# A hybrid diffusion block on one core: SyncE issues the modulation-piece transfers, TensorE sums their rows one tile later, and the last full down blocks are finished in pairs

## The reference

```python
ml = (silu(c) @ w_ada + b_ada).reshape(B, 9, D)          # nine modulation vectors, latent
mc = (silu(c_ctx)[None] @ w_ada + b_ada).reshape(1, 9, D) # the same for the context
h  = h  + 0.5*ml[:,2] * swiglu(modulate(rmsnorm(h,  g0), ml[:,0], ml[:,1]), ffn_w_in0, ffn_w_out0)
hc = hc + 0.5*mc[:,2] * swiglu(modulate(rmsnorm(hc, g0), mc[:,0], mc[:,1]), ffn_w_in0, ffn_w_out0)
# then: token mixing (pooling group and gated DeltaNet group), output projection,
# a second SwiGLU FFN on h alone, final RMSNorm
```

## Time and profile before

| What | Value |
|---|---|
| Median of three runs | 2981.55 us (2976.54 to 2985.0) |
| Profiled execution, its own time | 2979.76 us |
| Span of its trace | 2978.0 us |
| TensorE matmul busy | 2858.0 us, 96% of the span |
| VectorE busy | 1633.4 us, 55% |
| ScalarE busy | 968.1 us, 33% |
| GpSimd busy | 237.9 us, 8% |
| Mean granted TensorE clock | 0.977 |

### The profile page before, as it was taken

The page is one execution under the profiler, slowest core; times in us unless marked ns, Lnnn a source line. Parts: engine busy times, 40 slices in busy tenths (PEclk is TensorE's granted clock), DMA queues, the critical chain, the costliest instruction groups (busy, mean ns, idle before and its releaser), DMA issues. The chain is left out here.

```text
span 2978.0 us, 47625 instructions
## 1 busy us (share of the span) xinstructions
PE 2858.0 (96%) x17840; PEld 2496.2 (84%) x17840; DVE 1633.4 (55%) x2197; ACT 968.1 (33%) x1443; POOL 237.9 (8%) x388
## 2 busy tenths in 40 slices
PE   6999999999998999999999999998999999999998
PEld 3687777777877787888888888888999999999998
DVE  2556666666666663223222766665666555555555
ACT  2222221222212122111212555554444434443344
POOL 3000000000000000000101011546220000000001
PEclk8999999999999999999999999999999999999999
DMA  9765666667787874554554376686646555555554
GB/s 363 269 207 180 206 194 194 192 192 219 268 276 273 292 271 167 195 193 162 195 193 148 91 206 190 185 239 204 188 151 190 183 188 185 185 181 183 187 187 148
DMA packets 410321, 604.42 MB, mean 203 GB/s; under 512 B 52960, under 2 KB 303840, under 8 KB 401520
## 3 DMA queue, kind: packets, MB, share of 16 engines
q1 hardware_dynamic: 361536, 417.42, 44.4%
q10 hardware_dynamic: 48688, 185.73, 18.4%
HBM read 560.02 MB, written 43.02 MB: 203 GB/s over the span
## 5 line engine op out<-in xcount | busy, mean ns | idle before, releaser
L1929 DVE TENSOR_TENSOR wl<-raw,wh 128x1024 fp32r<-128x1024 f32 x638 | 781.4, 1231 | 997.6 <-ACT wh L1455 995.6
L1455 ACT CAST wh<-raw 128x1024 fp32r<-128x1024 f32 x638 | 664.7, 1047 | 1564.1 <-PE ps L760 1121.5
L759 PE MATMUL ps<-xl,wh 128*128 128x512 f32 (+1 forms) x2560 | 973.8, 380 | 0.0
L758 PE MATMUL ps<-xh,wh 128*128 128x512 f32 (+1 forms) x1904 | 728.1, 382 | 3.2 <-DVE xl L1980 2.5
L760 PE MATMUL ps<-xh,wl 128*128 128x512 f32 (+1 forms) x1904 | 720.8, 379 | 0.0
L759 PEld LDWEIGHTS ps<-xl,wh 128*128 128x128 f32 x2560 | 485.9, 190 | 90.8
L758 PEld LDWEIGHTS ps<-xh,wh 128*128 128x128 f32 x1904 | 362.2, 190 | 86.5 <-issue 15.8
L760 PEld LDWEIGHTS ps<-xh,wl 128*128 128x128 f32 x1904 | 361.2, 190 | 67.4
L758 PE MATMUL ps<-x2h,wh 128*128 128x256 f32 x1408 | 395.4, 281 | 1.7 <-DVE x2l L1980 1.7
L759 PE MATMUL ps<-x2l,wh 128*128 128x256 f32 x1408 | 393.8, 280 | 0.0
L760 PE MATMUL ps<-x2h,wl 128*128 128x256 f32 x1408 | 393.8, 280 | 0.0
(11 more groups left out here) (274 smaller groups left out, 2675.9 us busy)
## 6 DMA issues: line engine op xcount, KB each, us to landing
raw<-in_ffn_w_in SPq DMA_DIRECT2D x704, 256.0 KB, 3.3
raw<-in_ffn_w_out SPq DMA_DIRECT2D x176, 512.0 KB, 3.7
abuf<-in_w_ada ACTq DMA_DIRECT2D x64, 1024.0 KB, 7.1
abuf<-in_w_ada ACTq DMA_DIRECT2D x96, 512.0 KB, 4.2
xl<-d_h ACTq DMA_DIRECT2D x80, 512.0 KB, 3.3
ada_t<-in_ada SPq DMA_DIRECT2D x64, 512.0 KB, 9.1
raw<-in_w_in SPq DMA_DIRECT2D x128, 256.0 KB, 3.4
raw<-in_w_out SPq DMA_DIRECT2D x32, 512.0 KB, 4.5
```

Of the source, the lines that this page charges most:

```text
L758: mm(out, ah, bh, start=first, stop=False, skip_group_check=reopened)
L759: mm(out, ah, bl, start=False, stop=False, skip_group_check=reopened)
L1455: nc.scalar.copy(wh[:, t % HL, :], raw[:, t % RAW, :]).then_inc(hi_done, 1)
L1929: tt(tl, raw[:, t % RAW, :], th.bitcast(F32), ALU.subtract).then_inc(lo_done, 1)
```

## The change

Three things. (1) `load_piece` goes from ScalarE's stream to SyncE's: step x-1 of the running piece is issued behind weight tile x, and step 15 behind tile 0 of the next group (for the last piece, behind the first down tile). ScalarE's wait for the transfer of the hidden pair two back, in front of `hidden`, is replaced by a wait for the pair one back, in front of the next pair's transfer; only the last pair keeps one in front of `hidden`. (2) TensorE calls `reduce_rows` after tile 12 instead of 11, and `reduce_columns` after tile 14 instead of 13; VectorE's program is unchanged. (3) In the second half of the down projection blocks 0 and 1, then 2 and 3, are finished in pairs (`ff_both`): for each closing tile both blocks, and in the first pair the wait for a tile stands in front of that tile rather than in front of all.

```diff
--- before.py
+++ after.py
@@ -71,7 +71,6 @@
 PIECE_ONE = (N_MOD - 5) * D // (2 * HALF)
 PIECES = PIECE_BOTH + PIECE_ONE
 PIECE_AT = 12
-LOAD_AT = PIECE_AT - 2
 assert PIECES == GROUPS - 1
 
 
@@ -554,6 +553,25 @@
             def up_load(r, m, x):
                 load(r, UP_TILES, m * UP_TILES + x, up_source(0, r, m, *divmod(x, K_TILES)))
 
+            def load_piece(r, n, i):
+
+                sp.wait_ge(acc_done, steps(r, n, i - 1))
+                if n < PIECE_BOTH:
+                    src = w_ada_v[:, i, ds(r * HALF + (2 * D + n * HALF), HALF)]
+                    sp.dma_start(abuf[:, i % 2, 0, :], src).then_inc(abuf_in[i % 2], 16)
+                else:
+                    src = w_ada_v[:, i, ds(r * (2 * HALF) + (5 * D + (n - PIECE_BOTH) * 2 * HALF), 2 * HALF)]
+                    sp.dma_start(abuf[:, i % 2].rearrange("p s n -> p (s n)"), src).then_inc(abuf_in[i % 2], 16)
+
+            def up_loads(r, m):
+
+                for x in range(UP_TILES):
+                    up_load(r, m, x)
+                    if x:
+                        load_piece(r, m - 1, x - 1)
+                    elif m > 1:
+                        load_piece(r, m - 2, KT - 1)
+
             def ff_load(r, t, block, a):
 
                 sp.wait_ge(lo_done, tiles(r, HR, t))
@@ -575,13 +593,18 @@
                     up_load(0, 0, i - 3)
             for x in range(ADA_SS - 3, UP_TILES):
                 up_load(0, 0, x)
-            with sp.Fori(0, GROUPS - 1) as r:
-                for x in range(UP_TILES):
-                    up_load(r, 1, x)
+            up_loads(0, 1)
+            with sp.Fori(0, PIECE_BOTH - 1) as r:
+                up_loads(r, 2)
+            up_loads(0, PIECE_BOTH + 1)
+            with sp.Fori(0, PIECE_ONE - 1) as r:
+                up_loads(r, PIECE_BOTH + 2)
             for a in range(2):
                 t = T_DOWN + a * HALF_TILES
                 for i in range(HELD):
                     ff_load(0, t + i, SPILLED * 2 + i, a)
+                    if a == 0 and i == 0:
+                        load_piece(0, PIECES - 1, KT - 1)
                 with sp.Fori(0, (HALF_TILES - HELD) // HR) as r:
                     for b in range(HR):
                         ff_load(r, t + HELD + b, b, a)
@@ -910,13 +933,22 @@
                     n = ff_part(a, i, c, slice(0, NTOK))
                 n.then_inc(tile_used, 1)
 
-            def ff_whole(a, c, tiles_):
+            def ff_whole(c, tiles_):
                 for i in tiles_:
-                    n = ff_part(a, i, c, slice(0, NTOK), i == tiles_[-1])
-                    if a == 0 and c == 7:
+                    n = ff_part(0, i, c, slice(0, NTOK), i == tiles_[-1])
+                    if c == 7:
                         n.then_inc(tile_used, 1)
-                if a or c < 7:
+                if c < 7:
                     n.then_inc(down_done[0], 1)
+
+            def ff_both(c, tiles_):
+                for i in tiles_:
+                    if c == 0:
+                        ff_arrived(0, 1, i)
+                    for b in range(2):
+                        n = ff_part(1, i, c + b, slice(0, NTOK), i == tiles_[-1])
+                        if i == tiles_[-1]:
+                            n.then_inc(down_done[0], 1)
 
             def down():
                 pe.wait_ge(F[0]["hf_done"], 2 * GROUPS * PAIRS - 2)
@@ -930,10 +962,13 @@
                     for i in range(HALF_TILES - HR, HALF_TILES - close):
                         ff_tile(0, a, i)
                     closing_tiles = range(HALF_TILES - close, HALF_TILES)
-                    for i in closing_tiles:
-                        ff_arrived(0, a, i)
-                    for c in range(8 if a == 0 else 4):
-                        ff_whole(a, c, closing_tiles)
+                    if a == 0:
+                        for i in closing_tiles:
+                            ff_arrived(0, a, i)
+                        for c in range(8):
+                            ff_whole(c, closing_tiles)
+                for c in range(0, 4, 2):
+                    ff_both(c, closing_tiles)
                 for c in range(4, 8):
                     for i in closing_tiles:
                         n = ff_part(1, i, c, slice(0, SEQ), i == closing_tiles[-1])
@@ -992,9 +1027,9 @@
                         if p == 0 and m >= 2:
                             pe.wait_ge(red_out, r * 2 + 2 * (m - 1))
                     up_tile(0, r, m * UP_TILES + x, p, k)
-                    if x == PIECE_AT - 1:
+                    if x == PIECE_AT:
                         reduce_rows(r, m - 1)
-                    elif x == PIECE_AT + 1:
+                    elif x == PIECE_AT + 2:
                         reduce_columns(r, m - 1)
 
             def group(f, r, s, base, x_base):
@@ -1495,39 +1530,27 @@
                     i = fn(XH[n // 2][:, k, c_], ub[:, k % 2, c_], ACT.Identity, bias=SHIFT[n][s][:, k:k + 1])
                 i.then_inc(xh_done, 1)
 
-            def load_piece(r, n, i):
-
-                act.wait_ge(acc_done, steps(r, n, i - 1))
-                if n < PIECE_BOTH:
-                    src = w_ada_v[:, i, ds(r * HALF + (2 * D + n * HALF), HALF)]
-                    act.dma_start(abuf[:, i % 2, 0, :], src).then_inc(abuf_in[i % 2], 16)
-                else:
-                    src = w_ada_v[:, i, ds(r * (2 * HALF) + (5 * D + (n - PIECE_BOTH) * 2 * HALF), 2 * HALF)]
-                    act.dma_start(abuf[:, i % 2].rearrange("p s n -> p (s n)"), src).then_inc(abuf_in[i % 2], 16)
-
             def up_pairs(r, m, before=None):
 
                 for x in range(UP_TILES):
                     if before is not None:
                         before(x)
                     split(r, UP_TILES, m * UP_TILES + x + AHEAD)
-                    if x < LOAD_AT and m:
-                        load_piece(r, m - 1, x + KT - LOAD_AT)
-                    elif x >= LOAD_AT and m < GROUPS - 1:
-                        load_piece(r, m, x - LOAD_AT)
                     if x == 2 and m:
                         hidden_out(r, m, -1)
                     elif x == K_TILES + 2 and m < GROUPS - 1:
                         hidden_out(r, m, 0)
                     if x % K_TILES == K_TILES - 1:
                         p = x // K_TILES
-                        if m:
-                            act.wait_ge(hid_out, r * (64 * PAIRS // 2) + 32 * (2 * m + p - 1))
+                        if m == GROUPS - 1 and p:
+                            act.wait_ge(hid_out, 32 * SPILLED)
                         hidden(0, r, m, tiles(r, UP_TILES, m * UP_TILES + x), p, hth)
 
             def hidden_out(r, m, p):
 
                 n, b = 2 * m + p, 2 * (p % 2)
+                if n:
+                    act.wait_ge(hid_out, r * 64 + 32 * n)
                 act.wait_ge(F[0]["h_ready"], r * GROUP_FF + 2 * (n + 1))
                 rows = slice(2 * n, 2 * n + 2) if isinstance(r, int) else ds(r * GROUP_FF + 2 * n, 2)
                 for part, src in enumerate((hth, htl)):
```

## The result

| What | Before | After |
|---|---|---|
| Median | 2983.07 us (2976.54 to 2985.0, 4 runs) | 2894.84 us (2885.07 to 2896.22, 4 runs) |
| Ratio | | 0.9701, 95% interval 0.9674 to 0.9727 |
| Profiled execution: span | 2978.0 us | 2894.4 us |
| TensorE matmul busy | 2858.0 us, 96% | 2833.6 us, 98% |
| Mean granted TensorE clock | 0.977 | 0.990 |

The change takes 3.0% off. The prediction said 2896, within 2887 to 2920. The kernel before has one run more here than ahead of the prediction, which moves its median from 2981.55 to 2983.07 us.

What follows compares the result with a forecast made beforehand. A VectorE-ScalarE ring was taken to stall TensorE's row sums. Stalls and slow clock 79.7 plus closing 6.0 make 85.7 us off 2979.76, 2894.1; the median 1.79 higher, stated as 2896, range 2887 to 2920.

Steps and rivals of the forecast that it cites:

- The ring of step, issue, copy and split: Up projection: VectorE and ScalarE wait on each other, 5.33 us a tile beside TensorE's 5.44, so lateness reaches the row sums.
- Part 1: Up projection row sums: stalls and the slow clock behind them go, 79.7 us less.
- second limit: Piece transfers: two tiles must hold landing plus 2.64 us; 4.87 us a tile at 7.1 landing, slower than TensorE above 8.24.
- The term for the lower clock: Up projection: 23 us of the loss between first and last row sums is lower clock and the wait's own latency.
- Part 2: Side effects of moved transfers and later sums on SyncE, ScalarE and VectorE: covered, no cost expected.
- rival C: Up projection: the stall only moves with the later sums, 56 us come back, 2975.5 us; chance 0.03.
- Part 3: Closing of the down projection: pairs remove TensorE's 3.75 us gap and 2.3 us of slow matmuls, gain 6.0 us.
- A: Up projection: large pieces land late behind weights in SyncE's one queue, say 9.0 us, giving 2915 us; chance 0.11.
- B: Up projection: row and column sums themselves bring the lower clock, so 23 us stay, 2919 us; chance 0.04.
- D: Up projection: piece transfers land so late on SyncE, 10.0 us, that they set the pace, 3015 us; chance 0.02.

Runs made afterwards that it cites:

- opened in place: Kernel before with each piece transfer still issued by ScalarE but one tile later in its order, sums after tile 11 as before; 2899.25 us, ratio 0.9729.
- slowed by 0.65 us a tile: Kernel before with ScalarE's copy of a weight tile cut in eight from the second group on; 3054.33 us, ratio 1.0257.
- the run without later sums: Kernel before with the piece transfers moved to SyncE alone, sums after tiles 11 and 13, no closing pairs; 2902.43 us, ratio 0.9750.
- the run with half the lead: Changed kernel with each piece transfer waiting for the step right before it, not the one two before; 3108.85 us, ratio 1.0437.

## Why the prediction was right

**What bounds the kernel.** The ring of step, issue, copy and split is shown by three runs: opened on SyncE (2902), opened in place (2899), slowed by 0.65 us a tile (+74 us, with +79 us of wait at the sums).

**Part 1.** The working from the rows gave 79.7 us. From the end of tile 11 in the first group to the last sums it was 6.2 + 72.5 = 78.7: a period is 89.18, not 89.05, since row and column sums come with small delays around them (a start 0.32 instead of 0.23 us behind the last matmul of tile 12). The 0.6 us by which the last step should be ahead of the end of tile 11 are borne out for the small pieces by the run without later sums: 0.63. For the large pieces the text went by VectorE's 3.62 us a tile where its own second limit gives 4.87: 7.2 + 3 x 4.87 = 21.8 us, the very end of tile 11. There two of the four came 0.44 and 0.31 us late. What sets the closed ring back was only in part named: besides each `hidden` it is each pair of `hidden_out` issues in ScalarE's stream, which, twice a group, makes a tile of the ring 6.5 us instead of 5.33 (splits at 438.06 and 444.53 in the kernel before). The term for the lower clock (the larger part of 23 us) went in full with the idle that led to it.

**The second limit.** 8.24 us was right as a mechanism: the run with half the lead goes at the pace of the same sum. No run reaches 8.24 itself. 7.1 as the landing time on the other queue was right too. What I had wrong is the size of VectorE's waits: I called them short, and they are 22.4 us in 23 places, up to 3.1. The catching up runs into the limit just as the sum said (4.87 us a tile against 3.62), only more often than once a group. With the transfers on SyncE and the sums in their old places these waits are 10.2 us in 15 places; so about half of the 22.4 us came in with the later sums, which VectorE waits for.

**Part 2.** On TensorE nothing of the moved work shows. The cover of the later sums is needed for under 1 us; by itself it takes off 31 us, so rival C, that the stall moves with the sums, was about half right for a closed ring (3.7 us of 5.9 stayed) and does not matter with an open one.

**Part 3.** 6.3 us for 6.0. The text counted 13 matmuls from 1612.87 to 1618.11 where the trace has 12; the slow clock then cost 5.24 - 12 x 0.2267 = 2.5 us rather than 2.3, and the sum is 6.3. That the fetch of the last hidden tile was the real releaser shows in the run with the transfers on SyncE alone, where the same wait is put down to it:

```profile
PE ps L781 <- DMA xl<-d_h: 3.4, 1, 3.4
```

**The sum.** By spans it is 2978.0 - 2894.4 = 83.6 for 85.7: 0.5 lost before the first sums (tile 11 ends at 247.5 instead of 247.0), 1.1 in the periods, 0.9 behind the norm sums, 0.3 won in the closing. The 0.9 us behind the norm sums was not looked into. That the median came within 1.2 us of 2896 is partly luck: four runs of the changed kernel spread over 11 us.

**The rivals.** A did not come: the pieces land as before. The Trainium skill, "DMA: Bandwidth & Descriptors", section "Rules for kernel authors", says that spreading transfers over issuing engines brings no bandwidth, only issue time. The trace agrees: 298 GB/s from 695 to 1055 us with the pieces on either queue, and 7.1 or 7.0 us for a large piece. By its rule on queue rows, named in the prediction, I had looked for the cost at the piece. What became later is the weight tile, 3.7 to 4.9 us, and it does so with the pieces on ScalarE's queue as well. The order within one queue is not needed for it. B did not come: sums without a stall keep the full clock. The row it was argued from, 3.14 us of idle and full clock behind it, was no safe ground, as the last section shows. D needed 9.5 us of landing everywhere; the run with half the lead shows what that would have looked like.

The text gave SyncE's move the credit for opening the ring. It is one way of two, and the smaller edit does it as well.

## What to carry to other kernels

When an engine issues a transfer whose buffer another engine must free first, look at what stands behind that issue in its stream: a wait there can close a ring through both engines, and its period, not either engine's busy share (33% and 55% here), sets how fast lateness is made good. Issue the transfer one step later in the same stream, or from an idle engine, and check the landing time against the lead that is left. Giving a late result more room by moving its reader is worth less than it seems when the producer's next round starts after that reader.

## What the hardware showed that was not expected

- Eight copies of 128 x 128 on ScalarE took 1.70 us together, about 0.21 each, where I had worked out 0.30 from operations of 256 columns started 0.39 us apart.
- The same idle did not always bring the lower clock: in the run with later sums, 3.72 us ahead of the second sums and 1.93 us for them, 3.70 ahead of the third and 1.12. Nor did less idle always keep the full clock: 3.14 us kept it in the kernel before, 2.45 us did not in the run with the closing pairs alone, with matmuls 0.23 us apart up to the gap:

```profile
1130.94 1.94 PE L826 MATMUL ps<-acc,cols 128*32 128x512 f32 x8 [2.45 <-DVE acc L2104]
```

- The landing of a 1024 KB transfer follows neither the queue nor the density of the traffic alone. At 298 to 300 GB/s the medians were 7.1 us (changed kernel, SyncE), 7.0 (all three parts on ScalarE), 6.7 (SyncE alone) and 6.2 (later issue on ScalarE). At 244 GB/s, with the ring made slower, it was 6.8. At 220 GB/s in the run with half the lead, where no two pieces are under way together, it was 4.9. No run separates these causes.
